# VectorE makes each one-hot group two blocks earlier in its own order of work

## The chip, the cores and the metric

The kernel runs on one core of a Trainium2 chip. The metric is the device time of one execution in microseconds (us), as the median of several runs. The core has five engines with a queue each: TensorE (PE in the profile, with its weight loads as PEld), VectorE (DVE), ScalarE (ACT), GpSimd (POOL) and SyncE (SP), which here only issues transfers. The engines wait for one another through semaphores.

## The reference, cut to what matters

Two transformer blocks over 256 tokens of width 1024. The change lies in the last part of the second block, a layer of single-neuron experts (PEER) with 16384 = 128 x 128 experts:

```
q = tok @ w_q ;  s = q . sub_keys                    # two scores over 128 keys for each of 8 heads
s_top, i_top = top_k(s, 16); best, pos = top_k(sums of pairs, 16)
expert = i_row * 128 + i_col ;  gate = softmax(best)  # 8 x 16 = 128 experts for each token
act = gelu(u_emb[expert] . tok) * gate
out = sum_k act[k] * v_emb[expert[k]]
```

The kernel doesn't gather experts. It computes `u . tok` for all 128 expert blocks of 128 experts each, multiplies by a dense gate table that is zero for the experts that a token did not choose, and multiplies by all of `v`.

## The kernel before, in words

Weights stream from HBM in pages of 1 MB, two pieces a page, into a ring of three pages (SP, `page`, `next_page`, L371). Each piece is split in two parts: ScalarE writes the high half (`high`, L1233), VectorE the low half (`low`, L1704 to 1709), and TensorE multiplies with both in 24 matmuls (`up`, all matmuls are recorded at L496). ScalarE's high half of a piece may start once TensorE has begun the piece two before it. The split pieces lie in three buffers.

The stage that the change touches runs over n = 0 to 55, the 56 `u` blocks 16 to 71 (the first 16 are done before it, unsplit). I call it the up stage, and one n a block.

- TensorE: `up(n)` for each block; behind those with n at least 8 and (n - 8) mod 3 below 2 follows `quad(q)`, 32 in all. A quad makes the dense gates of four tokens of the second half (tokens 128 to 255) as four products of a one-hot matrix of rows and a weighted one-hot matrix of columns. It waits until VectorE has made these (`oh_ready`, L1171) and until ScalarE has copied out the quad two before it (`g_sb`, L1173).
- VectorE: `low` for each block, and `onehots(q)` (L2498 to 2507), one comparison over 128x512 (L2502) and four of 128x128 (L2505), into two buffers in turn. It waits until TensorE has done the quad two before it.
- ScalarE: for each even n the high halves of blocks n + 2 and n + 3, then for each block the GELU out of PSUM (`gelu`, recorded at L1260), which also gives TensorE its accumulator back, and behind a quad the copy into the table `G` (L1672).

The gates of the first 128 tokens come another way: GpSimd scatters them in 128 indirect DMAs (`scatter`, L474) into a table in HBM. They go in eight heads of 16, and a head starts only when all of the head before has landed. In SP's queue, ahead of the first transfers of this table back into SBUF, stands one wait for all 128:

```
            for p in range(UPS + RING, PEER + 2):
                next_page(p)
            sp.wait_ge(S["scat"], 2048)
            for m in range(RING):
                gate_in(m)
```

Behind them in the same queue stand the weight pages from the third of the next stage on. In that next stage (the down stage) VectorE multiplies each block's activations with its gates (`gate(e)`, L2530 to 2535, waiting for the transfer at `g_in`), and TensorE alternates `down(k)` with `up(72 + k)`. `down(0)` needs `gate(0)`, and TensorE takes its queue in order.

In VectorE's loop before, the one-hot group that belongs to block p stands behind `low(p + 2)`. TensorE needs it behind `up(p)`.

Of the kernel before, what the change touches and what calls it, by code (L numbers as in the profile page):

```python
# [50 lines left out]
def piece_no(p):  # L51

    return 2 * (p - SPLIT0) if p < WHOLE0 else 2 * (p - SPLIT0 - NWHOLE)
# [57 lines left out]
def build(nc, t, out):  # L111
    with ExitStack() as ctx:
# [368 lines left out]
        def _(pe):  # L481
# [376 lines left out]
            for k in range(8):  # L858
                _, m = three(ps[0:36, T % 2, 0:L], (w_if[0][:, k, :], w_if[1][:, k, :]), (h[0][:, k, :], h[1][:, k, :]),
                             k == 0, k == 7)  # L860
# [832 lines left out]
        def _(dve):  # L1693
# [10 lines left out]
            def low(p, s, i=0):  # L1704

                c = piece_no(p) + s
                dve.wait_ge(S["hi_ready"], c + 1 + 2 * LOOP * i)
                TT(piece[:, 1, c % 3], ring[:, p % RING, s], piece[:, 0, c % 3].bitcast(F32),  # L1708
                   ALU.subtract).then_inc(S["lo_ready"], 1)
# [75 lines left out]
            for q in range(2):  # L1785
                p = 2 * q
# [710 lines left out]
            UPS, PEER = PAGE["ups"], PAGE["peer"]  # L2497
            def onehots(q):  # L2498
                r, c = row_hot[q % 2], col_hot[q % 2]
                if q >= 2:  # L2500
                    dve.wait_ge(S["g_mm"], q)
                TT(r, iota.unsqueeze(1).to_broadcast([P, 4, P]),  # L2502
                   selT[:, 0, 4 * q:4 * q + 4].unsqueeze(2).to_broadcast([P, 4, P]), ALU.is_equal)
                for n in range(4):
                    ins = TS(c[:, n, :], iota, selT[:, 1, 4 * q + n:4 * q + n + 1], selT[:, 2, 4 * q + n:4 * q + n + 1],  # L2505
                             ALU.is_equal, ALU.mult)
                ins.then_inc(S["oh_ready"], 1)

            NU = AHEAD - EARLY
            for n in range(NU + 2):  # L2510
                if n < NU:
                    low(UPS + n // 2, n % 2)
                p = n - 2
                if p == 6:
                    dve.wait_ge(S["g_sb"], 1)
                if p >= 8 and (p - 8) % 3 < 2:
                    onehots(2 * ((p - 8) // 3) + (p - 8) % 3)

            def gate(e):
                m, b = e // 2, e % 3  # L2520
# [180 lines left out]
```

## Time and profile before

| | us |
|---|---|
| median of 3 runs | 1709.88 (1709.38 to 1711.42) |
| the profiled execution, its own time | 1711.12 |
| its span | 1709.4 |
| TensorE busy in the span | 1621.8 (95%) |
| VectorE / ScalarE / GpSimd busy | 1129.2 / 754.5 / 281.6 |
| mean granted TensorE clock | 0.99 of full |

All times in rows are from the span's start. An engine's busy time leaves out waits. Matmuls are pipelined, and a row of several counts to the modelled end of the last. "[... <- X]" is the idle time in front of an instruction and who ended it.

### The profile page before, as it was taken

To read this page: it belongs to the slowest core of one execution; us is meant where nothing else is said; L and a number is where in the kernel's file an instruction comes from. 1 tells how busy PE (TensorE), PEld (TensorE's weight loads), DVE (VectorE), ACT (ScalarE), POOL (GpSimd) and SP (SyncE) were. 2 spreads that over 40 slices of the span, in tenths; PEclk is the share of its full clock that TensorE was granted. 3 is DMA by queue.
4 is the path that set the end of the run, shared out by engine and by line. 5 is a ranking of instruction groups with operands and counts; after the bars stand their busy time and mean duration, and the time that the engine had idled before them with its cause. 6 is when DMAs were issued, how large, how long until landed. Compare 5 with 4: busy or idle time off the path is not lost.

```text
span 1709.4 us, 30317 instructions
## 1 busy us (share of the span) xinstructions
PE 1621.8 (95%) x12331; PEld 1485.5 (87%) x12331; DVE 1129.2 (66%) x2226; ACT 754.5 (44%) x1042; POOL 281.6 (16%) x224
## 2 busy tenths in 40 slices
PE   8999999999999999989999977778999999999998
PEld 3999969999999998879898877777999999988887
DVE  4746756777745779547697445455666666678887
ACT  2423535566635584324223444444444444443333
POOL 0000000022200001200077777760000000000000
PEclk9999999999999999999999999999999999999999
DMA  8866414466654443205255644443555555566664
GB/s 313 307 258 222 173 33 165 176 251 237 254 183 148 148 149 123 76 3 195 102 122 151 181 115 108 115 105 118 195 204 200 194 206 190 201 218 212 214 216 145
DMA packets 75833, 295.96 MB, mean 173 GB/s; under 512 B 24016, under 2 KB 40528, under 8 KB 41296
## 3 DMA queue, kind: packets, MB, share of 16 engines
q1 hardware_dynamic: 52832, 263.21, 43.9%
q0 software_dynamic: 21888, 25.24, 6.3%
q10 hardware_dynamic: 1008, 6.05, 0.9%
q8 instruction: 72, 1.18, 0.3%
q14 instruction: 33, 0.27, 0.0%
HBM read 284.97 MB, written 9.50 MB: 172 GB/s over the span
## 4 chain that ended last, share of the span: by engine, by line
PE 80%; DVE 11%; ACT 5%; issue 2%; DMA 1%; DVEq 0%; POOL 0%; SPq 0%; POOLq 0%
PE ps L496 80%; DVE piece L1708 4%; ACT piece L1233 3%; DVE late L2502 1%; DVE late L2505 1%; DVE row_more L2505 1%; DMA ring<-in_stream 1%; DMA arena<-in_xT 0%; DVE arena L1758 0%; ACT arena L1272 0%; DVE arena L1811 0%; ACT arena L1591 0%; ACT L1268 0%; DVE arena L1775 0%; DVE arena L1828 0%
## 5 line engine op out<-in xcount | busy, mean ns | idle before, releaser
L1708 DVE TENSOR_TENSOR piece<-ring,piece 128x1024 fp32r<-128x1024 f32 x432 | 531.3, 1238 | 414.9 <-ACT piece L1233 392.8
L496 PE MATMUL ps<-h_r,piece 128*128 128x256 f32 x5616 | 703.9, 285 | 4.4 <-DVE piece L1708 3.5
L496 PEld LDWEIGHTS ps<-h_r,piece 128*128 128x128 f32 x5616 | 690.4, 193 | 14.8 <-issue 8.7
L1233 ACT ACTIVATE piece<-ring 128x1024 fp32r<-128x1024 f32 x432 | 453.1, 1057 | 450.4 <-PE ps L496 445.7
L496 PE MATMUL ps<-piece,late_r 128*128 128x512 f32 x1536 | 359.0, 390 | 2.0 <-DVE late_r L2535 2.0
L496 PEld LDWEIGHTS ps<-piece,late_r 128*128 128x128 f32 x1536 | 284.7, 188 | 58.9 <-issue 2.2
L474 POOL DMA_INDIRECT gate_table<-early x128 | 213.5, 1668 | 201.0 <-DVE early L2417 125.6
L1260 ACT ACTIVATE arena<-ps 128x256 f32<-128x256 f32 (+1 forms) x163 | 71.4, 438 | 256.5 <-PE ps L496 251.9
L496 PE MATMUL ps<-arena,ring 128*128 128x256 f32 x512 | 111.9, 379 | 1.6 <-DVE arena L1775 1.6
L496 PEld LDWEIGHTS ps<-arena,ring 128*128 128x128 f32 x512 | 96.7, 190 | 14.8 <-issue 2.0
L496 PE MATMUL ps<-arena 64*64 64x64 f32 (+7 forms) x930 | 87.3, 296 | 7.7 <-DVE arena L2244 1.8
L496 PEld LDWEIGHTS ps<-arena 64*64 64x64 f32 (+4 forms) x930 | 68.5, 161 | 22.2 <-issue 10.4
L496 PE MATMUL ps<-ffn_hi,piece 128*128 128x256 f32 x352 | 63.5, 283 | 1.2 <-DVE piece L1708 1.2
L496 PEld LDWEIGHTS ps<-ffn_hi,piece 128*128 128x128 f32 x352 | 54.9, 192 | 1.4 <-DVE piece L1708 1.4
L2535 DVE TENSOR_TENSOR late_r<-arena,late_r 128x256 fp32r<-128x256 f32 x120 | 51.1, 426 | 4.1
L427 POOL TENSOR_TENSOR arena<-arena 128x256 f32<-128x256 f32 x22 | 16.3, 740 | 208.3 <-DVE arena L2033 208.3
L1672 ACT ACTIVATE arena<-ps 128x512 f32<-128x512 f32 x32 | 35.3, 1103 | 33.1 <-PE ps L496 33.1
L496 PE MATMUL ps<-ffn_lo,piece 128*128 128x256 f32 x176 | 49.8, 283 | 0.0
L496 PE MATMUL ps<-mg_hi,piece 128*128 128x256 f32 x256 | 42.8, 284 | 0.5 <-DVE arena L1973 0.5
L496 PE MATMUL ps<-row_more,late 128*128 128x128 f32 x128 | 18.7, 290 | 24.8 <-DVE row_more L2505 24.8
L496 PE MATMUL ps<-piece,h_r 128*128 128x256 f32 x288 | 40.0, 302 | 0.0
L496 PEld LDWEIGHTS ps<-row_more,late 128*128 128x128 f32 x128 | 15.7, 193 | 27.9 <-DVE row_more L2505 27.9
(313 smaller groups left out, 1593.8 us busy)
## 6 DMA issues: line engine op xcount, KB each, us to landing
ring<-in_stream SPq DMA_DIRECT2D x240, 1024.0 KB
arena<-in_mod POOLq DMA_DIRECT2D x16, 1024.0 KB, 6.3
gate_table<-early POOLq DMA_DIRECT2D x8, 1024.0 KB, 6.5
early<-gate_table SPq DMA_DIRECT2D x64, 128.0 KB, 4.6
arena<-in_const ACTq DMA_DIRECT2D x1, 2256.0 KB, 10.5
gate_table<-early POOLq DMA_INDIRECT x128
arena<-in_const ACTq DMA_DIRECT2D x1, 1648.0 KB, 10.0
xres<-in_xT SPq DMA_DIRECT2D x1, 1024.0 KB, 5.0
```

Source lines behind the costliest of these rows:

```text
L427: g.tensor_tensor(v, ga[:, b, :], v, ALU.mult).then_inc(S["gated"], 1)
L474: g.indirect_dma_start(gtab[:, :], bass.IndirectOffsetOnAxis(ap=gidx[:, hh, k:k + 1], axis=0), gw[:, hh, k:k + 1], None, compute_op=ALU.ad ...
L496: mm_last[0] = nc.tensor.matmul(*args, **kw)
L1233: A(piece[:, 0, c % 3], ring[:, p % RING, s], ACT.Copy).then_inc(S["hi_ready"], 1)
L1260: A(dst, ps[:, T % 2, src], func, **kw).then_inc(acc_free[T % 2], 1)
L1672: A(G[:, :, 4 * q:4 * q + 4].rearrange("p e n -> p n e"), ps[:, 6 + q % 2, :].rearrange("p (n e) -> p n e", n=4), ACT.Copy).then_inc(S["g_ ...
L1708: TT(piece[:, 1, c % 3], ring[:, p % RING, s], piece[:, 0, c % 3].bitcast(F32), ALU.subtract).then_inc(S["lo_ready"], 1)
L2502: TT(r, iota.unsqueeze(1).to_broadcast([P, 4, P]), selT[:, 0, 4 * q:4 * q + 4].unsqueeze(2).to_broadcast([P, 4, P]), ALU.is_equal)
L2505: ins = TS(c[:, n, :], iota, selT[:, 1, 4 * q + n:4 * q + n + 1], selT[:, 2, 4 * q + n:4 * q + n + 1], ALU.is_equal, ALU.mult)
L2535: TT(a_r[:, 1, b, :], a_t, a_r[:, 0, b, :].bitcast(F32), ALU.subtract).then_inc(S["a_ready"], 1)
```

## The change

VectorE's loop in the up stage ran over n = 0 to 57 and made the group that belongs to block n - 2 behind `low(n)`. Now it runs over n = 0 to 55 and makes the group that belongs to block n behind `low(n)`. The wait for `g_sb` (the copied selection) stays at n = 8. The instructions, their number and their operands stay the same; only VectorE's order changes.

```
             NU = AHEAD - EARLY
-            for n in range(NU + 2):
-                if n < NU:
-                    low(UPS + n // 2, n % 2)
-                p = n - 2
-                if p == 6:
+            for n in range(NU):
+                low(UPS + n // 2, n % 2)
+                if n == 8:
                     dve.wait_ge(S["g_sb"], 1)
-                if p >= 8 and (p - 8) % 3 < 2:
-                    onehots(2 * ((p - 8) // 3) + (p - 8) % 3)
+                if n >= 8 and (n - 8) % 3 < 2:
+                    onehots(2 * ((n - 8) // 3) + (n - 8) % 3)
```

## Rows read from the trace of the kernel before

**Rows 1.** The page: busy time, share and instructions of each engine.
```profile
PE 1621.8 (95%) x12331; PEld 1485.5 (87%) x12331; DVE 1129.2 (66%) x2226; ACT 754.5 (44%) x1042; POOL 281.6 (16%) x224
```

**Rows 2.** Waits from 964 to 1192 us: us in total, times, longest.
```profile
PE ps L496 <- DVE row_more L2505: 24.8, 15, 2.1
PE ps L496 <- DVE late L2505: 22.1, 16, 1.6
```

**Rows 3.** Timeline, TensorE: start, us, instruction, count, idle before.
```profile
968.58 1.16 PE L496 MATMUL ps<-late 128*128 128x128 f32 x8 [1.43 <-DVE late L2505]
...
1017.41 7.31 PE L496 MATMUL ps<-h_r,piece 128*128 128x256 f32 x48
...
1027.07 3.12 PE L496 MATMUL ps<-h_r,piece 128*128 128x256 f32 x24
1031.50 1.16 PE L496 MATMUL ps<-row_more,late 128*128 128x128 f32 x8 [1.31 <-DVE row_more L2505]
1032.41 6.00 PE L496 MATMUL ps<-h_r,piece 128*128 128x256 f32 x48
...
1186.53 1.06 PE L496 MATMUL ps<-row_more,late 128*128 128x128 f32 x8
1187.34 3.11 PE L496 MATMUL ps<-h_r,piece 128*128 128x256 f32 x24
```

**Rows 4.** Timeline, ScalarE and VectorE around one group.
```profile
1027.47 1.06 ACT L1233 ACTIVATE piece<-ring 128x1024 fp32r<-128x1024 f32 x1 [4.25 <-PE ps L496]
...
1028.56 1.23 DVE L1708 TENSOR_TENSOR piece<-ring,piece 128x1024 fp32r<-128x1024 f32 x1 [2.46 <-ACT piece L1233]
1028.70 1.11 ACT L1672 ACTIVATE arena<-ps 128x512 f32<-128x512 f32 x1
1029.70 0.72 DVE L2502 TENSOR_TENSOR late<-pconst_sb,late 128x512 f32<-128x512 f32 x1
...
1030.34 1.10 DVE L2505 TENSOR_SCALAR row_more<-pconst_sb,late 128x128 f32<-128x128 f32 x4
```

**Rows 5.** Stretches: length, busy (instructions) of PE, PEld, DVE, ACT, POOL, PEclk, DMA share, GB/s.
```profile
122.00:126.00 4.00, 4.00 (x21) 4.00 (x20) 1.23 (x1) 0.30 (x1) 0.00 (x0) 0.50 0.41 168
...
1017.00:1020.40 3.40, 3.40 (x19) 3.40 (x18) 1.23 (x1) 2.32 (x3) 3.07 (x2) 0.50 0.24 0
...
1300.00:1680.00 380.00, 380.00 (x2093) 332.25 (x2092) 281.06 (x541) 156.54 (x175) 0.00 (x0) 1.00 0.60 208
```

**Rows 6.** Timeline, TensorE, in the half-clock stretch of rows 5 near 122 us.
```profile
120.59 5.47 PE L496 MATMUL ps<-piece,h_r 128*128 128x256 f32 x24
```

**Rows 7.** GpSimd's scatters: all from 963.8 to 1147 us, then single ones.
```profile
L474 POOL DMA_INDIRECT gate_table<-early x80 | 135.7, 1697 | 51.4 <-issue 40.3 <-DMA gate_table<-early 11.1
...
963.85 1.57 POOL L474 DMA_INDIRECT gate_table<-early  x1 [4.30 <-DMA gate_table<-early]
965.73 2.62 POOL L474 DMA_INDIRECT gate_table<-early  x1 [0.30 <-issue]
...
1037.26 2.21 POOL L474 DMA_INDIRECT gate_table<-early  x1 [2.24 <-DMA gate_table<-early]
...
1142.27 2.58 POOL L474 DMA_INDIRECT gate_table<-early  x1 [0.30 <-issue]
1145.15 1.56 POOL L474 DMA_INDIRECT gate_table<-early  x1 [0.30 <-issue]
```

**Rows 8.** Timeline, VectorE, in the time of the scatter at 1142.27.
```profile
1142.16 1.23 DVE L1708 TENSOR_TENSOR piece<-ring,piece 128x1024 fp32r<-128x1024 f32 x1 [2.46 <-ACT piece L1233]
```

**Rows 9.** SP's queue, and the gate transfers' median us to landing (last column).
```profile
1173.19 1.63 SPq L380 DMA_DIRECT2D early<-gate_table  x3
...
early<-gate_table SPq DMA_DIRECT2D x3, 128.0 KB, 4.8
```

**Rows 10.** Timeline, the way into the down stage.
```profile
1191.00 0.29 DVE L2530 TENSOR_TENSOR arena<-arena,early 128x128 f32<-128x128 f32 x1 [3.93 <-ACT early L1260]
...
1192.43 2.97 PE L496 MATMUL ps<-piece,late_r 128*128 128x512 f32 x12 [1.98 <-DVE late_r L2535]
```

## The prediction, made before the changed kernel ran

> **What bounds the kernel now.** I read the page's busy times first: TensorE is busy 95% of the span [rows 1], so time can only be won where it waits, and little elsewhere. From 1300 to 1680 us it is busy 380.00 of 380 us [rows 5]: what the change moves ahead of the down stage arrives at the end in full. Then I read the list of waits over the up stage: TensorE waits 24.8 + 22.1 = 46.9 us for VectorE's one-hot comparisons, in 31 waits [rows 2], about 1.5 us for nearly every one of the 32 quads. The timeline shows how. `up(n)` starts at 1027.07 and ScalarE can only then make the high half two blocks on (1027.47 to 1028.53), VectorE its low half (1028.56 to 1029.79), and behind it the one-hot group, 1029.70 to 1031.44; the quad starts at 1031.50 [rows 3, 4]. The one-hots need nothing of this chain. They merely stand behind that low half in VectorE's queue.
>
> Next I looked for what else must be ready when the up stage ends. `down(0)` starts at 1192.43, 1.43 us after `gate(0)` starts at 1191.00 [rows 10]; the gates' transfers were issued at 1173.19 and land 4.8 us later [rows 9], so they have some 13 us in hand today. But their issue waits for the whole scatter, whose last instruction starts at 1145.15 and ends at 1146.71 [rows 7]. The scatter is thus the second chain, 40 us or so behind the first one's end.
>
> **The change part by part.**
>
> *The waits at the quads.* What would the stage last if TensorE never waited? One block costs 6.00 - 3.12 = 2.88 us and a quad 1032.41 - 1031.50 = 0.91 us [rows 3]. From the first quad (968.58) to the last (1186.53) lie 46 blocks and 31 quads in 217.95 us; unstalled 46 x 2.88 + 31 x 0.91 = 160.7 us. The loss of 57.3 us is made of 45.5 us of waits (46.9 without the 1.43 ahead of the first quad), about 30 x 0.24 = 7.2 us of the pipeline's tail that each wait exposes (3.12 - 2.88), and three pairs of blocks at half clock, 7.31 instead of 6.00 us in the one shown, some 4.3 us together (there are three such) [rows 3, 5]. In the changed order the first quad is not waited for either, so it would start at 968.58 - 1.43 - 0.2 = 966.95 and the last at 1127.65.
>
> *Does the new order hold TensorE up elsewhere?* The group now stands ahead of `low(n + 1)`. I walked six blocks (the pattern of quads and of ScalarE's pairs repeats then) with TensorE running unstalled: ScalarE's high half 1.06 us, beginning 0.4 us after the block that frees it, low half 1.14 us to the next instruction, group 0.64 + 1.10 us, high half and GELU together 1.23 (1027.47 to the copy at 1028.70), copy of a quad 1.11 [rows 4]. With `up` starts at 0, 3.8, 7.6, 10.5, 14.3, 18.1, 21.0 us, groups are ready at 8.2, 12.9, 19.7 and 22.6, where the quads need them at 13.4, 17.2, 23.9 and 27.7; the tightest low half is ready at about 18 for 21.0. VectorE works without a pause for some 7 us there, but about 3 us stay in hand. Its wait for the quad two before is met by then: the low half just ahead of the group already needed a later block to have begun. ScalarE's work per three blocks is 3 x 1.23 + 2 x 1.11 = 5.9 us against TensorE's 3 x 2.88 + 2 x 0.91 = 10.5. So I cost the new position at nothing, hidden under matmuls; without that cover it would cost up to the 1.7 us of a group, the same as today's wait. The two empty turns taken from the loop cost nothing. SP's pages are asked for by the low halves, one per two blocks: 1 MB in about 7 us, 150 GB/s, where 208 GB/s run beside busy matmuls later [rows 5].
>
> *What is late next.* With no more than TensorE to wait for, `down(0)` would start 0.91 us after 1127.65 plus today's 1192.43 - 1187.34 = 5.09 us from the start of the last block [rows 3, 10]: at 1133.65. The scatter isn't done then. It began its head at 963.85, before the first one-hot group, so nothing earlier moves. Its 80 scatters from there are 135.7 us busy, 51.4 idle [rows 7]. An undisturbed one takes 1.56 us and 0.30 of issue; 80 x 1.56 = 124.8, so 10.9 us are lengthening. The lengthened ones start inside one of VectorE's long two-input instructions: the one at 1142.27 took 2.58 us and started 0.11 us into the low half of 1142.16 to 1143.39 [rows 7, 8]. Those instructions now come in 160.7 instead of 217.95 us, 1.36 times as dense, up to about 1130, and none behind it: 10.9 x 166/183 x 1.36 = 13.4, some 2.3 us more. The pauses between heads (2.24 us from the end of the last scatter to the next head [rows 7]) I leave as they are. So the scatter ends at 1146.71 + 2.3 = 1149.0, has landed at 1151.2, the gates land at 1156.0, and `down(0)` starts at 1157.4. TensorE will have been idle for some 25 us. In this trace the clock was at the lower of its two levels, 1.2 GHz, in stretches of about 3.4 us and up, and three of these lie in the up stage where TensorE had paused again and again; 24 matmuls at that level took 5.47 us [rows 5, 6] against 3.12, so I charge 2.4 us for one block after the pause.
>
> Sum: 1192.43 - 1157.4 - 2.4 = 32.6 us won. Of 58.8 that the new order frees, 26.2 are given back as one wait ahead of `down(0)`.
>
> The first pages behind the wait in SP's queue are no further cost: the third page of the down stage would be issued about 1153, and high halves want it some 6 us behind `down(0)`; a page lands in several us and there are about 10.
>
> *A rule against this change.* The lengthened scatter in rows 7 and 8 ran 1.02 us over, nearly what was left of VectorE's instruction. The Trainium skill, "SBUF — State Buffer", section "SBUF: two separate sides", states that VectorE and GpSimd take one shared port pair as an exclusive lock for a whole instruction, among others when VectorE has two SBUF inputs and GpSimd reads SBUF; this trace agrees in that row. By that rule a scatter can lose at most the rest of one such instruction. If the denser order made every scatter lose that much, this would be the third rival below; if it blocked none, the first.
>
> **The rivals.**
>
> *First: the scatter doesn't hold, TensorE does.* `down(0)` at 1133.65, without a cold restart: 58.8 us won, 1652.3 in the profile's terms, 1651 as a median. It needs the scatter's last instruction to end by 1133.65 - 1.43 - 4.8 - 2.2 = 1125.2, 21.5 us sooner. All lengthening gone gives 10.9, and the rest would have to come out of pauses. That happens only if most pauses are due to VectorE too. Partway, each us that the scatter gains is a us.
>
> *Second: the wait only moves.* If the group in front of `low(n + 1)` makes that low half late, TensorE waits there instead, up to 1.7 us for each of 32 groups, 54 us, and `down(0)` starts where it does today: 1710. Against it stand the 3 us in hand. And up to 23 us of such waits would hide behind the scatter.
>
> *Third, the other side: GpSimd is starved.* If VectorE's denser work lengthens all of the 79 scatters behind 963.85 to the 2.62 us of the longest row, the scatter ends 79 x 1.06 - 10.9 = 73 us later, at 1220, `down(0)` at about 1231 with the restart, and the time is 1711.1 + 38 = 1749. It turns slower than before once the last scatter ends after 1181.6, that is at a mean lengthening of (10.9 + 34.9)/79 = 0.58 us instead of 0.14. Against it: VectorE's two-input instructions fill under half of the time even unstalled (46 x 1.23 + 32 x 0.64 = 77 us in 161), and one starting inside them loses half of one on average.
>
> **How the numbers follow.** The profiled execution took 1711.1 us, 1.2 over the median. 1711.1 - 32.6 = 1678.5, as a median 1677.3. Forecast (scatter ends the stage): 80%, its own range 1669 to 1687, which is the scatter 6 to 8 us off and the restart at 0 to 5 us. First rival 8%, second 4%, third 3%; 5% for part of a gain between forecast and no change. Range 1662 to 1688: it reaches toward the first rival, since the pauses of the scatter are the part I can't price, and toward some starvation. A change under 0.2% can't be told from none here. Faster by more than that: 94% (forecast, first rival, part); within it: 3%; slower: 3%.
>
> **What would show it.** Right: the waits of TensorE for L2505 are gone or below 5 us; the three half-clock stretches in the up stage are gone; the last quad starts near 1128; TensorE has one idle time of about 20 to 27 us ahead of `down(0)`, whose chain goes through SP, the scatter and VectorE's `gate(0)`; the last scatter starts at 1145 to 1150; behind the restart one stretch at half clock; from `down(0)` on all as before. Wrong: waits for L1708 of more than 10 us in the up stage (second rival), scatters of over 1.8 us in the mean (third), or `down(0)` before 1145 (first).

## The result and the profile after

| | before | after |
|---|---|---|
| median, us | 1709.97 (1709.38 to 1711.42, 4 runs) | 1688.67 (1684.46 to 1691.9, 4 runs) |
| ratio | | 0.9873, 95% interval 0.9845 to 0.9900 |
| profiled execution, us | 1711.12 | 1686.05 |
| its span | 1709.4 | 1684.3 |
| its mean granted clock | 0.99 | 0.982 |

Faster by 21.3 us as a median, by 25.1 in the profiled executions; forecast were 32.6. The median lies 0.7 us above the upper end of the range. One of the four executions of `small_pages` below took 2260 us at a mean granted clock of 0.651; it is left out, and the median given for that kernel is of the other three.

First TensorE's timeline after the change (start, us, instruction, count, idle before), which answers to [rows 3, 10]:

```profile
968.59 3.12 PE L496 MATMUL ps<-h_r,piece 128*128 128x256 f32 x24
971.54 1.06 PE L496 MATMUL ps<-row_more,late 128*128 128x128 f32 x8
972.35 6.00 PE L496 MATMUL ps<-h_r,piece 128*128 128x256 f32 x48
...
1127.74 1.06 PE L496 MATMUL ps<-row_more,late 128*128 128x128 f32 x8
1128.55 3.11 PE L496 MATMUL ps<-h_r,piece 128*128 128x256 f32 x24
1164.85 5.45 PE L496 MATMUL ps<-piece,late_r 128*128 128x512 f32 x12 [33.18 <-DVE late_r L2533]
1170.10 3.05 PE L496 MATMUL ps<-h_r,piece 128*128 128x256 f32 x24
```

No quad is waited for any more: none of them has an idle time in front. The last starts at 1127.74 instead of 1186.53. Then TensorE stands for 33.18 us, and `down(0)` behind it takes 5.45 us instead of 2.97. The waits from 964 to 1192 us (us in total, times, longest), which answer to [rows 2]:

```profile
POOL gate_table L474 <- issue: 44.4, 76, 5.1
DVE arena L2528 <- DMA early<-gate_table: 35.1, 1, 35.1
...
PE ps L496 <- DVE late_r L2533: 33.2, 1, 33.2
```

31 waits of 46.9 us have become one of 33.2, and VectorE's `gate(0)` (L2528) waits for the transfer of the gates. Followed back, that is the scatter: SP issues this transfer 1.47 us after the last scatter's end. GpSimd's group of scatters from head 3 on (count, busy, mean ns, idle before and who ended it), and then the timeline of the end with SP's issue of the gates and the start of `gate(0)`, answer to [rows 7, 9, 10]:

```profile
L474 POOL DMA_INDIRECT gate_table<-early x80 | 142.8, 1785 | 56.6 <-issue 44.4 <-DMA gate_table<-early 12.2
```

```profile
1158.21 1.56 POOL L474 DMA_INDIRECT gate_table<-early  x1 [0.30 <-issue]
...
1161.24 1.41 SPq L380 DMA_DIRECT2D early<-gate_table  x3
...
1163.42 0.29 DVE L2528 TENSOR_TENSOR arena<-arena,early 128x128 f32<-128x128 f32 x1 [35.13 <-DMA early<-gate_table]
```

The last scatter starts 13.06 us later than before (1158.21 against 1145.15), though nothing in GpSimd's program changed. I split the time behind head 3's first scatter into three: 80 undisturbed scatters, *lengthening* (busy time over 1.56 us each), and *pauses* (idle time over 0.30 us each). Before: 11.0 us of lengthening, 23.4 of pauses. After: 18.1 and 28.5. Head 3 also began 0.84 us later. 7.1 + 5.1 + 0.8 = 13.0. Only part of the 5.1 us lies at the waits between two heads. The four that follow head 3 (scatters 64, 80, 96 and 112, counted from 0) grew by 1.3 us together; the stops at every 15th scatter inside the heads (60, 75, 90, 105, 120) by 1.2; and the stops at scatters 56 and 84 by 2.6.

The same stretch in both kernels, before first (length, busy of PE, PEld, DVE, ACT, POOL with instructions, PEclk, DMA share, GB/s), and after it the stretch of the wait:

```profile
964.00:1127.00 163.00, 128.25 (x1010) 123.58 (x1009) 79.58 (x149) 68.40 (x92) 120.00 (x71) 0.98 0.48 115
```

```profile
964.00:1127.00 163.00, 163.00 (x1379) 163.00 (x1379) 107.64 (x202) 93.75 (x125) 117.85 (x64) 1.00 0.56 149
1127.00:1160.00 33.00, 4.67 (x40) 4.46 (x38) 1.23 (x1) 2.73 (x5) 24.97 (x16) 0.64 0.19 0
```

In 163 us TensorE does 1379 matmuls instead of 1010, VectorE is busy 107.6 us instead of 79.6, the pages move 149 GB/s instead of 115, and GpSimd gets 64 scatters through instead of 71. Behind the last quad, in the wait, it does 16 in 33 us.

### The profile page after: what moved, and what is told of

It reads as the page before. It is cut to its first block, busy times and chain, and to the rows that moved or that the text cites. A ratio compares the mean times of both kernels' runs of the same rounds, so it can differ in the third digit from the quotient of the medians.

```text
span 1684.3 us, 30316 instructions
## 1 busy us (share of the span) xinstructions
PE 1612.9 (96%) x12331; PEld 1482.8 (88%) x12331; DVE 1128.8 (67%) x2226; ACT 754.5 (45%) x1042; POOL 288.2 (17%) x224
## 4 chain that ended last, share of the span: by engine, by line
PE 70%; POOL 12%; DVE 6%; issue 5%; ACT 3%; DMA 3%; POOLq 0%; DVEq 0%; SPq 0%
PE ps L496 70%; POOL gate_table L474 12%; DMA gate_table<-early 2%; DVE piece L1708 1%; DMA ring<-in_stream 1%; ACT piece L1233 1%; DMA arena<-in_xT 0%; DVE arena L1758 0%; ACT arena L1272 0%; DVE arena L1811 0%; ACT arena L1591 0%; ACT L1268 0%; DVE arena L1775 0%; DVE arena L1828 0%; DVE arena L1940 0%
## 5 line engine op out<-in xcount | busy, mean ns | idle before, releaser
L496 PE MATMUL ps<-piece,late_r 128*128 128x512 f32 x1536 | 361.5, 392 | 33.2 <-DVE late_r L2533 33.2
L474 POOL DMA_INDIRECT gate_table<-early x128 | 220.2, 1721 | 205.1 <-DVE early L2417 124.1
L2528 DVE TENSOR_TENSOR arena<-arena,early 128x128 f32<-128x128 f32 x120 | 34.0, 284 | 35.1 <-DMA early<-gate_table 35.1
L496 PEld LDWEIGHTS ps<-piece,h_r 128*128 128x128 f32 x288 | 39.0, 211 | 0.8 <-issue 0.8
```

The costliest lines, as they stand in the source:

```text
L474: g.indirect_dma_start(gtab[:, :], bass.IndirectOffsetOnAxis(ap=gidx[:, hh, k:k + 1], axis=0), gw[:, hh, k:k + 1], None, compute_op=ALU.ad ...
L496: mm_last[0] = nc.tensor.matmul(*args, **kw)
L2528: TT(a_t[:, 0:P], a_t[:, 0:P], z, ALU.mult).then_inc(S["a_chain"], 1)
```

## The experiments

A number that helps in all of them: the time of a profiled execution minus the start of its last scatter. If the scatter ends the stage and all behind it stays the same, this is a constant.

| kernel | last scatter starts | lengthening | pauses | profiled execution | minus last scatter | median | ratio to before (95%) |
|---|---|---|---|---|---|---|---|
| before | 1145.15 | 11.0 | 23.4 | 1711.12 | | 1709.97 | |
| after | 1158.21 | 18.1 | 28.5 | 1686.05 | 527.8 | 1688.67 | 0.9873 (0.9845 to 0.9900) |
| again | 1156.19 | 16.6 | 28.5 | 1682.61 | 526.4 | 1684.7 | 0.9855 (0.9839 to 0.9870) |
| one_block | 1166.59 | 24.3 | 28.5 | 1693.78 | 527.2 | 1690.99 | 0.9878 (0.9855 to 0.9901) |
| part20 | 1166.24 | 16.9 | 33.2 | 1693.13 | 526.9 | 1687.62 | 0.9866 (0.9848 to 0.9885) |
| low_halves | 1156.47 | 11.7 | 32.6 | 1683.97 | 527.5 | 1683.82 | 0.9814 (0.9790 to 0.9837) |
| low_quarters | 1157.30 | 12.4 | 31.7 | 1684.82 | 527.5 | 1678.16 | 0.9818 (0.9801 to 0.9834) |
| small_pages | 1147.46 | 19.0 | 19.8 | 1675.31 | 527.9 | 1671.87 | 0.9780 (0.9760 to 0.9799) |
| small_scratch | 1181.20 | 18.0 | 38.0 | 1708.47 | 527.3 | (one run) | |
| warm | 1165.26 | 17.0 | 29.2 | 1691.91 | 526.7 | 1684.98 | 0.9852 (0.9834 to 0.9869) |
| pulled | 1161.20 | 17.6 | 28.9 | 1682.18 | 521.0 | 1681.67 | 0.9827 (0.9810 to 0.9845) |
| best | 1148.59 | 8.6 | 28.1 | 1669.88 | 521.3 | 1674.07 | 0.9779 (0.9762 to 0.9797) |
| before_quarters | 1142.32 | 4.9 | 26.8 | 1721.94 | | 1722.64 | 1.0062 (1.0038 to 1.0085) |
| half_scatter | 1000.02 | | | 1651.31 | | 1653.02 | 0.9676 (0.9660 to 0.9692) |

Lengthening and pauses are summed over the 80 scatters from head 3 on, from GpSimd's timeline. One profile is one execution, and the medians come from several, so the two need not agree to a few us (low_quarters: its profiled execution was the slowest of four). The start of head 3 moves too, from one execution to another: 964.69 and 964.10 in the two profiles of the changed kernel, 972.08 in `warm`, whose program is the same up to there. So a last scatter some us earlier or later in one profile says little by itself; the columns of lengthening and pauses are free of this part.

**The changed kernel again, and how far ahead the group must be.** `again` has no edit. `one_block` puts each group behind the low half one block on, here against the kernel before:

```
+            def behind(q):
+                return 8 + 3 * (q // 2) + q % 2 + (1)
...
-                if p >= 8 and (p - 8) % 3 < 2:
-                    onehots(2 * ((p - 8) // 3) + (p - 8) % 3)
+                for q in range(32):
+                    if behind(q) == n:
+                        onehots(q)
```

> The changed kernel once more, for a second profile beside the kernel before on one chip. Theory (the scatter ends the stage, and VectorE's long two-input instructions lengthen it): the first profile of the changed kernel had its last scatter start at 1158.21 us and down(0) at 1164.85; the four times of it spread over 7.4 us where the four of before spread over 2.0. So here too one idle stretch of TensorE ahead of down(0), last scatter at 1155 to 1168, down(0) 5 to 8 us behind it, time 1684 to 1692, and time minus last scatter constant within 1.5 us over the two profiles. Rival (the spread comes from later, in the down stage): time minus last scatter differs by several us.

> Each one-hot group stands behind the low half one block ahead, not two. Theory (the stage is ended by the scatter, and the distance matters only until the quads are no longer waited for): the group is ready about 4.3 us after the start of up(n-1), the quad wants it 2.9 + 2.9 us after, so no waits at the quads, last quad starts at 1127 to 1129 as in the changed kernel, time within 4 us of it (1684 to 1692). Rival (two blocks are needed): waits of TensorE for L2505 of some 10 to 25 us in the up stage; even then the time stays near that of the changed kernel as long as the stage ends before 1155.

`again` ran at 0.9855 with its last scatter at 1156.19, and time minus last scatter was 526.4 against 527.8: as the theory has it. One premise of that text did not hold: the kernel before, timed 11 times there, spread over 6.9 us itself, so the spread is no mark of the change. `one_block` had no wait at a quad, its last `up` block of the stage started at 1124.94, and it stood 45.16 us ahead of `down(0)`; its ratio overlaps that of the change. One block would have done. Its last scatter was 8.4 us later than in the first profile of the change: 2.2 us of that lie ahead of head 3, and 6.2 are lengthening, 24.3 us in all, the most of any kernel. Only 25 of its scatters began inside a low half, but they lost 0.89 us each on average. Some lost more than was left of the low half, as this one (GpSimd's line first, then VectorE's):

```profile
994.81 3.04 POOL L474 DMA_INDIRECT gate_table<-early  x1 [0.31 <-issue]
994.60 1.22 DVE L1708 TENSOR_TENSOR piece<-ring,piece 128x1024 fp32r<-128x1024 f32 x1
995.73 0.68 DVE L2502 TENSOR_TENSOR late<-pconst_sb,late 128x512 f32<-128x512 f32 x1
```

It ran 1.48 us over, with 1.01 us left of the low half when it began; the two-input comparison that follows at once ends at 996.41. Six scatters of this profile lost 1.48 us or more. Others with the same instructions behind them lost only the rest of the low half (the one at 992.12: 0.83 of 0.93 us), and what decides between the two is open.

**Is it the scatter alone?** Half of the scatters left out:

```
-            scatter(0, 128)
+            scatter(0, 64)
...
-            sp.wait_ge(S["scat"], 2048)
+            sp.wait_ge(S["scat"], 1024)
```

> The changed kernel without the scatters of heads 4 to 7 (64 of 128, their gates are left out of the table), SP waits for the 64 alone. Theory (the scatter ends the stage): the scatter is done near 1002, so down(0) follows TensorE's own chain, 5.1 us behind the start of the last block at about 1128 to 1129: down(0) at 1133 to 1135, no long idle stretch and no half clock behind it, time 1652 to 1657. Rival (something else, such as the pages behind SP's wait or VectorE, keeps down(0) late): idle stretch of over 5 us stays, time above 1660.

TensorE's timeline of it:

```profile
1127.39 3.11 PE L496 MATMUL ps<-h_r,piece 128*128 128x256 f32 x24
1132.48 2.97 PE L496 MATMUL ps<-piece,late_r 128*128 128x512 f32 x12 [1.98 <-DVE late_r L2533]
1135.28 3.04 PE L496 MATMUL ps<-h_r,piece 128*128 128x256 f32 x24
```

`down(0)` came at 1132.48, 5.09 us behind the start of the last block exactly as in the kernel before [rows 3, 10], at full clock, and the time was 1653.0. So nothing but the scatter stood between the change and 1653: the medians differ by 35.7 us. (This kernel's table lacks half of the gates of the first 128 tokens.)

**What lengthens a scatter?** Low halves of the up stage in two instructions (shown), and later in four (steps of 2 in place of 4):

```
-                low(UPS + n // 2, n % 2)
+                low_parts(UPS + n // 2, n % 2)
...
+                for a in range(0, 8, 4):
+                    ins = TT(piece[:, 1, c % 3, a:a + 4, :], ring[:, p % RING, s, a:a + 4, :],
+                             piece[:, 0, c % 3, a:a + 4, :].bitcast(F32), ALU.subtract)
```

> In the up stage each low half of 128x1024 is made by two instructions of 128x512, nothing else changes. Theory (a scatter that starts inside a two-input instruction of VectorE is held until that instruction ends): in the changed kernel 35 of 80 scatters started inside a low half and ran 16.9 us over in all; with instructions of half the length a held scatter loses half as much, so the lengthening falls from 18.1 to about 10 us, the last scatter starts about 8 us sooner (near 1150), the time is 5 to 9 us less than the changed kernel. Rival (held until VectorE's whole work is done, or lengthened by something else such as the weight pages' traffic): lengthening stays near 18 us and the time within 2 us of the changed kernel.

> Each low half of the up stage in four instructions of 128x256. In halves the lengthening was 11.7 us against 16.6 and 18.1. Theory (a scatter is held to the end of one instruction): about 7 to 9 us of lengthening, of which the low halves' share falls again by half while that of the 128x512 comparison (about 3 us) stays; the time gains 0 to 4 us on the version in halves. Rival (the hold passes on to the next instruction in the queue when these stand close): no less than in halves, or more.

In the changed kernel two scatters in a row, with VectorE beside them:

```profile
1078.74 1.23 DVE L1708 TENSOR_TENSOR piece<-ring,piece 128x1024 fp32r<-128x1024 f32 x1 [1.68 <-ACT piece L1233]
...
1079.06 2.37 POOL L474 DMA_INDIRECT gate_table<-early  x1 [0.30 <-issue]
...
1081.52 1.22 DVE L1708 TENSOR_TENSOR piece<-ring,piece 128x1024 fp32r<-128x1024 f32 x1
1081.73 2.44 POOL L474 DMA_INDIRECT gate_table<-early  x1 [0.30 <-issue]
```

The first starts 0.32 us into a low half that ends at 1079.97, 0.91 us on, and takes 2.37 - 1.56 = 0.81 us too long. The second has 1.01 us of its low half ahead and takes 0.88 too long. Of the 80 scatters 31 began inside a low half, and 16.8 of the 18.1 us of lengthening are theirs; before it were 23 and 9.8 of 11.0. (The 35 in the text above counts four more, which began up to 0.04 us ahead of a low half and lost nothing.) The six that began inside one of the short one-input comparisons (L2505) lost nothing.

With the low half in two instructions the lengthening was 11.7 us, in four 12.4, against 18.1 and 16.6. `low_quarters` is faster than the change by more than the intervals (0.9818 against 0.9855 and 0.9873; its interval ends at 0.9834, theirs begin at 0.9839). `low_halves` is less clear: its ratio is given as 0.9814, but its median is only 0.9 us under that of `again`, measured beside it, and the gain lies in two of its five executions (1672.6 and 1676.2). Nor did four parts bring less lengthening than two. A low half takes 1.43 us in four parts, not 1.23, and so covers more of the time. Another reason is in the trace of `low_quarters` (GpSimd's line first, then VectorE's):

```profile
1020.76 2.64 POOL L474 DMA_INDIRECT gate_table<-early  x1 [0.31 <-issue]
1020.55 1.42 DVE L2514 TENSOR_TENSOR piece<-ring,piece 128x256 fp32r<-128x256 f32 x4
```

This scatter began 0.21 us into the first quarter and lost 1.08 us, three times the 0.36 us of a quarter: it was held through the others as well. Five scatters lost 1.08 us or more there, 5.6 of the 12.4 us, and three of `low_halves` lost 0.94 or 0.95, the whole pair. Most others lost no more than the rest of one part. So shorter instructions shorten the hold of most scatters, but the theory that a scatter is always released at the end of one instruction is wrong, and the rival in the text of `low_quarters` is right for these five. The last scatter of the profiled executions was not 8 us sooner, since their pauses were 3 to 4 us longer; why is open.

The Trainium skill, "SBUF — State Buffer", section "SBUF: two separate sides", has a cause for such a hold: VectorE and GpSimd share a pair of ports, and one of them takes it as an exclusive lock for a whole instruction. The trace of the changed kernel agrees, in that its two scatters shown above lost nearly what was left of a two-input instruction (0.81 of 0.91 us, 0.88 of 1.01).

**What makes the pauses?** First the pages' traffic, cut to 64 KB a page in the up stage (the blocks then multiply with what is left in the ring):

```
-                next_page(p)
+                if p < UPS + 4 or p >= PEER:
+                    next_page(p)
+                else:
+                    ...
+                    sp.dma_start(ring[:, p % RING, 0, 0], t["stream"][p][:, 0:P]).then_inc(loaded[p % RING], 16)
```

> The changed kernel with the weight pages of the up stage (from its fifth to its last) cut from 1 MB to 64 KB (the blocks then multiply with what is left in the ring). Order, waits and compute instructions stay. The pauses between scatters beyond 0.30 us of issue came to 28.5 us behind head 3 in both profiles of the changed kernel and 33.2 and 32.6 in two variants of it, 23.4 in the kernel before; the pages' traffic there was 149 GB/s against 115. Theory (the pauses wait for scatters to land, and the pages' traffic on the same transfer engines delays that): pauses fall to 8 to 16 us, lengthening stays at 16 to 18, last scatter 12 to 20 us sooner, at 1137 to 1146, time 1666 to 1674. Rival (the pauses have a fixed length, or VectorE makes them): they stay at 25 to 33 us, time as the changed kernel's.

```
-SCRATCH = 4096
+SCRATCH = 2048
```

> The changed kernel with 2048 instead of 4096 bytes for GpSimd's store of descriptors. Pauses beyond the ones between heads came at scatter 15, 30, 45, 60, 75, 90, 105 and 120 in every profile. Theory (the store holds 15 scatters and GpSimd waits until old ones have landed): pauses at every 7th scatter, 18 in all instead of 8, of 1.6 us and up each, the last scatter 8 to 20 us later, time 1694 to 1706. Rival (these pauses come from the instructions' own loading): they stay at every 15th.

The stretch of small_pages and one pause of it, and the same pause (ahead of scatter 75, counted from 0) in the changed kernel:

```profile
964.00:1127.00 163.00, 163.00 (x1379) 163.00 (x1378) 107.77 (x202) 93.75 (x125) 124.41 (x68) 1.00 0.25 22
```

```profile
1026.60 1.73 POOL L478 DMA_INDIRECT gate_table<-early  x1 [1.87 <-issue]
```

```profile
1034.40 1.55 POOL L474 DMA_INDIRECT gate_table<-early  x1 [5.10 <-issue]
```

With 22 GB/s in place of 149 and everything else the same, lengthening stays at 19.0, pauses fall from 28.5 to 19.8, and the time by 13 to 17 us. The direction is the expected one, the size is smaller: pauses of 8 to 16 us and a last scatter at 1146 at the latest were expected. Every pause but one of this profile behind head 3 is between 1.8 and 2.3 us, while in the changed kernel the same ones reached 5.10, 3.91 and 3.72. So the traffic of the pages makes the pauses longer; that VectorE makes this difference is ruled out, since its work was the same (107.77 against 107.64 us busy). The page's "issue" at them is no issue. The end of small_scratch:

```profile
1149.73 1.56 POOL L474 DMA_INDIRECT gate_table<-early  x1 [2.61 <-issue]
...
1164.46 1.55 POOL L474 DMA_INDIRECT gate_table<-early  x1 [1.96 <-issue]
...
1179.34 1.56 POOL L474 DMA_INDIRECT gate_table<-early  x1 [2.12 <-issue]
1181.20 1.56 POOL L474 DMA_INDIRECT gate_table<-early  x1 [0.30 <-issue]
```

Pauses now stood at scatters 7, 14, 21 and so on to 126 instead of 15, 30, 45: with half the store GpSimd stops twice as often. So these are waits for room. That room comes when earlier scatters have landed fits this and small_pages, but no trace shows it directly. The last scatter was 23.0 us later and the time 1708.5, more loss than expected: 13.6 of the 23.0 are there when head 3 starts, and 9.5 are longer pauses behind it. There are further pauses at 28, 56, 84 and 112, in every kernel that has these scatters; with the small store all four are also multiples of 7, so it doesn't tell them apart. What they are is open.

**The cold restart, and work for the wait.** `warm` lets TensorE do eight small products when the scatter has landed. `pulled` moves the first two `u` blocks of the down stage, which need no gates, ahead of `down(0)`. `best` is both with low halves in quarters.

```
+            pe.wait_ge(S["scat"], 2048)                 # warm, best
+            pe.wait_ge(S["g_sb"], 33)
+            for k in range(8):
+                mm(ps[:, 6, 0:P], ident, ident, start=True, stop=True)
             for k in range(2):
-                both(k)
+                up(AHEAD + k, C1 + k)                    # pulled, best
+            for k in range(2):
+                down(k, C1 + 2 + k)
...
-    for e in range(P - AHEAD):
+    blocks += [u[AHEAD], u[AHEAD + 1], v[0], v[1]]
+    for e in range(2, P - AHEAD):
```

> The changed kernel; TensorE does eight 128x128 fp32 products into a free bank when the last scatter has landed, in the 3 to 5 us in which the gates are transferred. Theory (down(0) runs 2.5 us longer because the clock is at its lower level behind the idle stretch): down(0) takes 2.9 to 4.0 us instead of 4.5 to 5.5, time 1 to 2.5 us less than the changed kernel. Rival (the first down block is long for another cause, such as weights not yet split): down(0) stays at 4.5 to 5.5 us at full clock.

> The changed kernel with the first two u blocks of the down stage (72 and 73) placed ahead of down(0) and down(1), in the weight stream and in the engines' order. They don't need the scattered gates. Theory (the stage is ended by the scatter, TensorE stands idle 33 us ahead of down(0)): two blocks of 2.88 us go into the idle stretch, it shrinks to about 27 us, down(0) starts when it did, and the time is 4.5 to 6 us less than the changed kernel's, 1678 to 1682. Rival (the next weight page, which stands behind the wait in SP's queue, is then late for down(2)): a new wait of 2 us or more behind down(1) takes back part, gain under 3 us.

> All that won: low halves of the up stage in four instructions each, the two u blocks ahead of down(0), and eight small products while the gates are transferred. Theory: 5.8 for the blocks, 1.9 for the clock, 4 to 7 for the shorter lengthening, together 11 to 14 us below the changed kernel: 1671 to 1676 as a median, with a spread of some 7 us. Rival (the parts hide one another): no better than the best of them alone, about 1678.

TensorE's timeline of warm, of pulled and of best, in this order:

```profile
1168.33 3.78 PE L496 MATMUL ps<-pconst_sb 128*128 128x128 f32 x16 [35.10 <-DMA gate_table<-early]
1171.86 3.60 PE L496 MATMUL ps<-piece,late_r 128*128 128x512 f32 x12
```

```profile
1125.89 8.87 PE L496 MATMUL ps<-h_r,piece 128*128 128x256 f32 x72
1167.80 10.22 PE L496 MATMUL ps<-piece,late_r 128*128 128x512 f32 x36 [33.04 <-DVE late_r L2535]
```

```profile
1151.77 3.78 PE L496 MATMUL ps<-pconst_sb 128*128 128x128 f32 x16 [14.19 <-DMA gate_table<-early]
1155.31 6.22 PE L496 MATMUL ps<-piece,late_r 128*128 128x512 f32 x24
1162.67 3.06 PE L496 MATMUL ps<-piece,late_r 128*128 128x512 f32 x12 [1.14 <-DVE late_r L2547]
```

With the small products ahead `down(0)` takes 3.60 us instead of 5.45: the extra time was the clock's. In the times this 1.9 us is not to be seen (0.9852 against 0.9855), and time minus last scatter fell by 1 us at most. But 1691.91 is 2.7 us more than the span of this execution, 1689.2, where it is 1.7 to 1.8 us more in the other eight. By spans, span minus last scatter is 523.9 in `warm`, against 524.7 in `again`, 526.1 in the first profile and 525.6 as the mean of the eight: a gain of 0.8 to 2.1 us, in which the 1.9 can lie. `pulled` won its own length: three blocks run as one piece of 8.87 us, and time minus last scatter is 521.0, 6.2 us below the mean of the others, 527.2; its median is 3 to 7 us under the change's two. `best` reached 1674.07, ratio 0.9779, inside the 1671 to 1676 expected, and beats both kernels. It shows the next wait: `down(2)` stands 1.14 us for its gated activations (L2547). VectorE makes these behind a low half that waits for ScalarE's high half, and ScalarE had waited 3.52 us for the page, which is behind the scatter's wait in SP's queue.

**Two attempts that tell something by failing.** `part20` leaves the last 12 groups in their old places, `before_quarters` makes the low halves of the kernel before in four instructions.

> The first 20 one-hot groups stand two blocks sooner as in the changed kernel, the last 12 where they were before. TensorE's own way: last quad at 1127.7 + 12 x 1.75 (the wait and its tail) + up to two half-clock losses of 1.4 = 1149 to 1152, down(0) by TensorE's chain at 1155 to 1158. Theory (lengthening by density of VectorE's two-input instructions): in the last 12 groups the scatter runs at the rate of before, so it ends 2 to 5 us sooner than in the changed kernel; the idle stretch ahead of down(0) shrinks from 33 to under 12 us; time 1 to 6 us less than the changed kernel. Rival (the density has nothing to do with it): the scatter ends as in the changed kernel and the time is the same within 1 us.

> The kernel before with the low halves of the up stage in four instructions of 128x256. Theory (the lengthening of the scatters costs time only where the scatter ends the stage): lengthening falls from 11 to 6 to 9 us and the time does not fall; it rises by 0 to 6 us, since each low half takes about 0.15 us longer and stands ahead of the one-hot group for which TensorE waits. Rival (the lengthening or the low half's form matters to the time by another way): the time falls by over 3 us.

`part20` waited at quads again in its last third, as it should (its last quad came at 1145.56), but it stood 23.26 us ahead of `down(0)` where under 12 were expected; its lengthening was 16.9, its pauses 33.2 and its time the same as the change's. The gain of a thinner last third was not found, and the theory of that text missed. Its last scatter in the profile is 8.0 us later than the change's, of which 4.6 lie ahead of head 3. In `before_quarters` the waits at the quads grew (us in total, times, longest):

```profile
PE ps L496 <- DVE row_more L2505: 28.7, 15, 2.5
...
PE ps L496 <- DVE late L2505: 25.3, 16, 1.8
```

That is 54.0 us instead of 46.9; lengthening fell from 11.0 to 4.9, the last scatter came 2.8 us sooner, and the time rose by 0.6%. The same edit wins 6 us or more where the scatter is the bound and loses where VectorE's group is. (10.2 us of loss at the median, against 1712.43 beside it, is more than the 7.1 of waits; it was expected at 0 to 6.)

## Why the prediction was right or wrong, point by point

| step | forecast | measured |
|---|---|---|
| last quad starts | 1127.65 | 1127.74 |
| head 3 starts | 963.85 | 964.69 |
| more lengthening | 2.3 | 7.1 |
| longer pauses | 0 | 5.1 |
| last scatter starts | 1147.45 | 1158.21 |
| its end to the gates' issue | 2.2 | 1.47 |
| issue to `gate(0)` | 4.8 | 2.18 |
| `gate(0)` to `down(0)` | 1.43 | 1.43 |
| `down(0)` starts | 1157.4 | 1164.85 |
| slower restart | 2.4 | 2.48 |
| won, profiled executions | 32.6 | 25.1 |

- The waits at the quads, and that the new order makes no other: right to 0.1 us at the last quad. The three half-clock stretches are gone too (PEclk 1.00 above).
- What is late next: right. The scatter ends the stage; half_scatter gives 1653.0 where the first rival was put at 1651, and the nine profiles with all scatters and no moved block have the time minus the last scatter within 1.5 us (526.4 to 527.9), though that scatter starts up to 33.7 us apart in them.
- The size of the scatter's own delay: wrong, and this is the step that failed. The sum moved the last scatter by 2.3 us; it moved by 13.1, of which 7.1 are lengthening, 5.1 pauses and 0.8 come from ahead of head 3. So two terms were mis-sized by nearly the same: the pauses by 5.1 us, the lengthening by 7.1 - 2.3 = 4.8.
- The first term is the pauses. "The pauses between heads ... I leave as they are" put them at nothing, and they cost 5.1 us. Most of the pauses do not even lie between heads. small_pages shows that the pages' traffic lengthens them, and the pages now come 1.3 times as fast; I had checked the pages' rate only for the pages' own sake. By kind, 1.3 us are waits for a head to land, 1.2 are waits for room, and 2.6 came at scatters 56 and 84, where what GpSimd waits for is open.
- The second term is the lengthening: right in cause, too small. I scaled it by the density of VectorE's instructions over the part of the time in which they run, 1.24 times (the 10.9 to 13.4 of the text is 2.5 us, not the 2.3 that went into the sum). Measured were 18.1/11.0 = 1.65 times. The low halves that begin between head 3's first scatter and the last scatter's end are 47 instead of 38, 1.24 times as well, so the density was right. But 31 instead of 23 scatters began inside one, and each of them lost 0.54 instead of 0.42 us. So it is a matter of where in a low half a scatter starts, and density does not give that: `one_block`, as dense, had 25 of them at 0.89 us each.
- "By that rule a scatter can lose at most the rest of one such instruction" is refuted too: in `one_block` a scatter with 1.01 us left lost 1.48. In the changed kernel no scatter with more than 0.03 us left of a low half lost more than that, so the forecast did not fail by this.
- The way from the last scatter to `down(0)`: 3.3 us too long. I took the landing time of gates that were moved beside a page [rows 9]; with SP's queue held by the wait, none was under way (0 GB/s in the stretch above), and the three gate transfers landed in 2.3 us at the median instead of 4.8.
- The restart: right. A stretch at 1.2 GHz behind the wait, `down(0)` 2.48 us longer.
- 10.8 too early at the scatter, 3.3 too late behind it: 7.5 us, which is 32.6 - 25.1. The other 3.8 us of the 11.4 between forecast and median are the difference between one profiled execution (1686.05) and the median of four (1688.67), and between 1711.12 and 1709.97 before.
- The rivals: the first is refuted by its condition (the scatter didn't end sooner), the second by the timeline, the third in its size: the mean lengthening rose to 0.23 us, not 0.58. But its direction was the real one, and the forecast gave it 3%.

## What to carry to other kernels

When a wait is taken away, the next chain is not only late by what it was late before: it runs beside busier engines and transfers now, and its own pauses have to be priced as waits with a cause, not copied. An operation that is ordered earlier may cost its own engine nothing, and still cost another engine something; look at each engine whose instructions grow longer beside it. And where one chain has become the end, work that does not need it can be placed in the wait at its full length.

## What the runs showed of the hardware that I had not expected

- GpSimd's indirect scatters stop at every 15th with 4096 bytes of store and at every 7th with 2048. Behind head 3 the stops at every 15th last 1.8 to 2.0 us with 22 GB/s of other traffic, and 1.8 to 5.1 us with 149 (up to 5.5 in `again`).
- A two-input VectorE instruction of 128x1024 holds a scatter that starts in it to nearly its end (0.81 of 0.91 us left, 0.88 of 1.01); the six scatters of the changed kernel that began in instructions of 128x128 with one tensor input lost nothing.
- Where two-input instructions follow one another closely, the hold can go on through the next: 1.48 us lost with 1.01 left in `one_block`, 1.08 us lost over quarters of 0.36 in `low_quarters`.
- A 128 KB transfer of the gates landed in 2.3 us at the median with nothing beside it, against 4.8 us beside a page.
